# Where GpSimd takes the fifth weight block of a feed-forward period: ahead of the split of the down slot, or behind it

## The chip, the cores and the metric

The kernel runs on one core of one Trainium2 chip. The metric is the device time of one execution in microseconds. Float32 data are used throughout; TensorE multiplies them as pairs of a high and a low part.

## What is computed

Two transformer-like blocks in a row on a 1024 x 1024 activation `x` (tokens x model width). The change lies in the feed-forward part of the first block:

```python
h = rmsnorm(x, norm2_g[l])
u = h @ w_ffn_up[l]                      # 1024 -> 2 x 2816
a, b = u[..., :D_FF], u[..., D_FF:]
a = causal_dwconv(a, ffn_conv_w[l], ffn_conv_b[l])   # three taps
x = x + (jax.nn.silu(a) * b) @ w_ffn_down[l]         # 2816 -> 1024
```

Ahead of it stand an RWKV scan and an mLSTM, behind it the attention layers of the second block. They take most of the span and the change doesn't touch them.

## The kernel before

`build` writes one program per engine; semaphores order them. Data stand transposed, with channels on the 128 partitions. Each fp32 product is made of three matmuls: high part times high part, high times low, low times high. So each weight tile must be split ahead of its use: a copy rounded to the matmul's type is the high part, and the original less the high part is the low part.

The feed-forward part has 22 tiles of 128 hidden channels. Tile 0 is done apart; then come 21 periods, f = 1 to 21 (`FFN_ROWS`). Twenty of them are in loops with four periods per turn (`LOOP_TILES`), the last is written out. In period f TensorE does the up product of tile f (`up_pair`, its matmuls are L1260) and then the down product of tile f-1 (`ffn_down`, L1290).

The up product of a tile (a and b columns together, a 2 x 2 block product) is made with seven half-size products instead of eight (Strassen's scheme). Each of the seven needs one weight block of 128 x 512, which is either a loaded quarter (`upA`, `upB`, two halves each) or a sum or difference of quarters (`unit_sum`). The blocks are called units 0 to 6 in the code. Unit 4, the fifth, is `upB[:, 0, :]`, which holds a difference since line 642 was done. For each unit ScalarE writes the high part (`unit_high`, L2099) and GpSimd the low part (`unit_low`, L630). Both go to a ring of four buffers, so unit 4 goes where unit 0 was, and `unit_high` for unit 4 waits until TensorE is done with product 0. On ScalarE it stands behind `seed` (L2105), which copies bank A to bank B, also after product 0.

TensorE takes the products in the order 0 to 6, 12 matmuls of 512 columns each. It waits for `up_lo` before each of them, for `c_seeded` ahead of product 4 (VectorE's L3088, which itself waits for product 2), and for `ae_added` ahead of product 6 (L3107).

The down weights of a tile (128 x 1024, the "down slot") are loaded to `wraw[:, 1, :]` and split by GpSimd in `down_split`: L662 writes the high part, L664 the low part. `down_split(f)` waits until the down product that used these buffers before is done (`down_done`). That is the last thing that TensorE does ahead of period f's up product. What it writes is used by the down product at the end of period f.

GpSimd's order in period f is: `down_split(f)`, then `later_units(f)` (unit 4, the sum for unit 5 on L653, units 5 and 6), then `first_units(f + 1)` (units 0 to 3 of the next tile, with three sums and differences of the loaded quarters, L640, L642, L644).

VectorE's order in period f: second and third tap of tile f-1's convolution (L3036 and L3039, scalar_tensor_tensor over `apad` and `aconv`), the scaling of b (L3073), the seed of bank C (L3088), the gating product (L3078), the low part of the gated tile (`gL`, L3082), then the exits of banks B, A/E and C (L3101, L3107, L3115), and 16 additions of the down product to `xT` (L2986). ScalarE's order: `seed`, unit 4's high part, SiLU (L2138), `shared_product` (L2111), unit 5's high part, the gated tile's high part `gH` (L2142), unit 6's high part, the next tile's first three, the first tap (L2116), a copy of bank A, the next tile's unit 3.

SyncE's queue issues the loads in a fixed order (`ffn_period`): the down slot once `down_ready` counts the split; half 0 of `upB` once unit 4's low part is done; both halves of `upA` once the sum for unit 5 is done; half 1 of `upB` once unit 6's low part is done.

Of the kernel before, what the change touches and what calls it, by code (L numbers as in the profile page):

```python
# [31 lines left out]
FFN_ROWS = FFN_TILES - 1  # L32
# [92 lines left out]
def build(nc, xin, vec, w_lora, consts, cmask, rope, lnm, band, ws, park, out):  # L125
    with ExitStack() as ctx:
# [11 lines left out]
        def since(name, n):  # L138
            return n + LATER[name][1]

        def sem(name):
            if name in LATER:
                name = LATER[name][0]
            if name not in sems:
                sems[name] = ctx.enter_context(nc.semaphore(name))
            return sems[name]
# [186 lines left out]
        def ring_at(q, u):  # L333

            return (UNITS * q + u) % RING
# [102 lines left out]
        def _(sp):  # L438
# [25 lines left out]
            for j in range(2):  # L464
                rate, keys, power, _, scratch = SETS[j]
                sp.dma_start(AR[:, 0, j, :], keys[:, :]).then_inc(sem("x_moved"), 16)
                sp.dma_start(AR[:, 1, j, :], power[:, :]).then_inc(sem("x_moved"), 16)
                sp.dma_start(BK[:, j, :, CH:3 * CH], rate[:, :].rearrange("p (c x) -> p c x", x=2 * CH)
                             ).then_inc(sem("x_moved"), 16)
                for e in range(2):  # L470
                    sp.dma_start(key_part(j)[:, :, e, :], pairs_of(scratch)[:, :, e, :]).then_inc(sem("x_moved"), 16)
# [67 lines left out]
        def _(pool):  # L539
# [84 lines left out]
            def unit_low(f, q, u):  # L624

                s = ring_at(q, u)
                src = (upA[:, 0, :], unit_sum[s][:, :], upA[:, 0, :], upA[:, 1, :], upB[:, 0, :], unit_sum[s][:, :],
                       upB[:, 1, :])[u]
                pool.wait_ge(sem("up_hi"), since("up_hi", f * UNITS + (u + 1 - UNITS)))
                pool.tensor_tensor(unit_lo[s][:, :], src, unit_hi[s][:, :], ALU.subtract).then_inc(sem("up_lo"), 1)  # L630

            def first_units(f, q):

                n = f * UNITS - UNITS
                unit_low(f, q, 0)
                pool.wait_ge(sem("up_A21"), since("up_A21", f * 16))
                pool.wait_ge(sem("up_A22"), since("up_A22", f * 16))
                pool.wait_ge(sem("up_used"), since("up_used", n + 2))
                s1 = unit_sum[ring_at(q, 1)]
                pool.tensor_tensor(s1[:, :], upB[:, 0, :], upB[:, 1, :], ALU.add).then_inc(sem("up_sum"), 1)  # L640
                pool.wait_ge(sem("up_sum"), since("up_sum", f * 4 - 3))
                pool.tensor_tensor(upB[:, 0, :], upA[:, 0, :], upB[:, 0, :], ALU.subtract).then_inc(sem("up_sum"), 1)  # L642
                pool.wait_ge(sem("up_sum"), since("up_sum", f * 4 - 2))
                pool.tensor_tensor(upA[:, 0, :], s1[:, :], upA[:, 0, :], ALU.subtract).then_inc(sem("up_sum"), 1)  # L644
                unit_low(f, q, 1)
                unit_low(f, q, 2)
                unit_low(f, q, 3)

            def later_units(f, q):

                unit_low(f, q, 4)
                pool.wait_ge(sem("up_used"), since("up_used", f * UNITS - 1))
                pool.tensor_tensor(unit_sum[ring_at(q, 5)][:, :], upA[:, 1, :], upA[:, 0, :], ALU.subtract  # L653
                                   ).then_inc(sem("up_sum"), 1)
                unit_low(f, q, 5)
                unit_low(f, q, 6)

            def down_split(f):

                pool.wait_ge(sem("down_raw"), since("down_raw", f * 16))  # L660
                pool.wait_ge(sem("down_done"), since("down_done", f))
                pool.tensor_tensor(wH[:, 1, :], wraw[:, 1, :], zero, ALU.add).then_inc(sem("down_hi"), 1)  # L662
                pool.wait_ge(sem("down_hi"), since("down_hi", f))
                pool.tensor_tensor(wL[:, 1, :], wraw[:, 1, :], wH[:, 1, :], ALU.subtract).then_inc(sem("down_ready"), 1)  # L664
# [6 lines left out]
            with pool.Fori(0, (FFN_ROWS - 1) // LOOP_TILES) as i:  # L671
                for q in range(LOOP_TILES):
                    f = i * LOOP_TILES + (q + 1)
                    down_split(f)
                    later_units(f, q)
                    first_units(f + 1, q + 1)
            down_split(FFN_ROWS)
            later_units(FFN_ROWS, 0)
            pool.wait_ge(sem("down_raw"), since("down_raw", (FFN_ROWS + 1) * 16))
            pool.wait_ge(sem("up_used"), since("up_used", RING + FFN_ROWS * UNITS - 2))  # L680
# [26 lines left out]
        def _(pe):  # L707
# [803 lines left out]
            def pair_end(br, L, i, first):  # L1511

                _, transposes, values, _ = steps(br, L, i, first)

                def last_block():
                    transposes(7, 0)
                    values(6)

                def values_and_rows():
                    values(7)  # L1520
                    pe.wait_ge(sem("at_rec"), L * 8 + i + (first + 1))
                    pe.transpose(bank(4)[0:16, 0:P], stat[:, S_REC, :], ident).then_inc(sem("at_rows"), 1)

                at = (2, 4, 8) if br == "C" else (3, 6, 11)
                return {at[0]: last_block, at[1]: lambda: transposes(7, 1), at[2]: values_and_rows}
# [231 lines left out]
        def _(act):  # L1757
# [167 lines left out]
            def prepare_powers(j):  # L1925
                _, cum, power, inverse, _ = SETS[j]
                if j == 3:
                    act.wait_ge(sem("rp_done"), 2)
                act.wait_ge(sem("rp_cum"), j + 1)
                act.activation(power[:, :], cum[:, :], ACT.Exp, scale=-DECAY_SCALE).then_inc(sem("rp_exp"), 1)  # L1930
                act.activation(inverse[:, :], cum[:, :], ACT.Exp, scale=DECAY_SCALE).then_inc(sem("rp_exp"), 1)
# [1777 lines left out]
```

## Time and profile before

| what | value |
|---|---|
| median of 3 runs | 3469.43 us (3468.46 to 3472.11) |
| the profiled execution's own time | 3469.67 us |
| its span in the trace | 3467.6 us |
| mean granted TensorE clock | 0.984 of full |
| TensorE busy | 3306.3 us, 95% |
| GpSimd busy | 1395.1 us, 40% |
| VectorE busy | 1931.8 us, 56% |
| ScalarE busy | 927.0 us, 27% |
| L1260, L1290: share of the chain that ended last | 11%, 6% |

The profile is one execution. Its time is the span plus 2.07 us that lie around it. Times in rows are from the span's start. In a timeline a row gives the start, the duration, the engine (PE is TensorE, POOL GpSimd, DVE VectorE, ACT ScalarE, SP SyncE), the line, the operation and its tiles, and in brackets how long the engine idled before and what released it. Matmul durations are modelled and overlap (0.39 us each, started some 0.227 us apart), so TensorE's pace is read from starts.

### The profile page before, as it was taken

The page shows a single profiled execution, that of the slowest core. Times are in us where ns is not written, and L with a number is a line of the kernel's source. Part 1 is how long each engine was busy: PE and PEld are TensorE (multiplying, and loading weights), DVE is VectorE, ACT ScalarE, POOL GpSimd, SP SyncE. Part 2 cuts the span into 40 slices and gives each one's busy share as a digit, 9 for nine tenths or more (in the row PEclk, how much of TensorE's full clock was granted, in tenths as well). Part 3 has the DMA queues.
Part 4 walks back from the last instruction along what each step waited for, and adds up shares of the span by engine and source line. Part 5 has one row for each costly group of instructions (what it writes and reads, how often), then busy time and mean ns, then how long its engine had stood idle before and what let it go on. Part 6 is the DMA issues. An engine that isn't in the chain of part 4 may idle for free.

```text
span 3467.6 us, 55643 instructions
## 1 busy us (share of the span) xinstructions
PE 3306.3 (95%) x22310; PEld 2650.3 (76%) x22310; DVE 1931.8 (56%) x2588; ACT 927.0 (27%) x1515; POOL 1395.1 (40%) x719
## 2 busy tenths in 40 slices
PE   7999788999999999989999999999999999999997
PEld 6878688787888888767777678888776776788886
DVE  7445644558777788855544553443646544443433
ACT  4222343223333333332323320000333322300001
POOL 3323244137777777422222234444322222244444
PEclk9999899999999999999999999999999999999998
DMA  3121100311111111211111121111311111211111
GB/s 138 39 91 44 54 4 4 131 49 37 55 54 54 54 54 51 88 63 52 54 53 43 37 86 49 48 48 49 123 49 50 42 43 49 86 49 49 48 46 63
DMA packets 68390, 198.08 MB, mean 57 GB/s; under 512 B 11409, under 2 KB 22385, under 8 KB 66305
## 3 DMA queue, kind: packets, MB, share of 16 engines
q1 hardware_dynamic: 50880, 140.05, 11.9%
q10 hardware_dynamic: 17344, 55.63, 4.9%
q8 instruction: 128, 2.10, 0.3%
q14 instruction: 38, 0.30, 0.0%
HBM read 167.16 MB, written 16.96 MB: 53 GB/s over the span
## 4 chain that ended last, share of the span: by engine, by line
PE 87%; DVE 7%; issue 2%; ACT 2%; POOL 1%; DMA 1%; ACTq 0%; DVEq 0%; POOLq 0%; SPq 0%
PE ps L723 42%; PE ps L1260 11%; PE ps L1290 6%; PE ps L1662 5%; PE ps L1236 4%; PE ps L1444 3%; PE ps L1471 3%; PE ps L1489 3%; DVE sc L3325 2%; PE ps L1313 1%; PE ps L1035 1%; PE ps L1011 1%; PE ps L1398 1%; PE ps L1103 0%; DVE hL L2659 0%
## 5 line engine op out<-in xcount | busy, mean ns | idle before, releaser
L545 POOL TENSOR_TENSOR wH<-wraw,pv 128x1024 fp32r<-128x1024 f32 x175 | 343.7, 1964 | 1699.1 <-PE ps L723 1423.9
L723 PE MATMUL ps<-hH,wH 128*128 128x512 f32 x2128 | 671.4, 397 | 26.0 <-DVE hL L2659 11.5
L723 PE MATMUL ps<-hL,wH 128*128 128x512 f32 x2128 | 664.1, 393 | 0.0
L723 PE MATMUL ps<-hH,wL 128*128 128x512 f32 x2128 | 663.0, 393 | 0.0
L723 PEld LDWEIGHTS ps<-hH,wH 128*128 128x128 f32 x2128 | 394.6, 189 | 113.4 <-issue 17.8
L547 POOL TENSOR_TENSOR wL<-wraw,wH 128x1024 fp32r<-128x1024 f32 x175 | 461.0, 2634 | 13.8
L723 PEld LDWEIGHTS ps<-hL,wH 128*128 128x128 f32 x2128 | 398.4, 189 | 84.1 <-issue 1.7
L723 PEld LDWEIGHTS ps<-hH,wL 128*128 128x128 f32 x2128 | 398.1, 189 | 82.8 <-issue 0.3
L2986 DVE TENSOR_TENSOR xT<-ps,xT 128x512 f32<-128x512 f32 x544 | 367.2, 690 | 62.8 <-PE ps L1290 53.4
L3428 DVE TENSOR_TENSOR sg<-ps,mrows 128x1024 f32<-128x1024 f32 x46 | 56.3, 1224 | 360.4 <-PE ps L723 360.4
L2300 ACT ACTIVATE sc<-sc,stat 128x256 f32<-128x256 f32 (+7 forms) x256 | 171.1, 669 | 127.4 <-DVE stat L3332 66.4
L2402 ACT ACTIVATE sg<-sg 128x1024 f32<-128x1024 f32 x46 | 48.8, 1061 | 550.0 <-DVE sg L3428 550.0
L1444 PE MATMUL ps<-kP,qP 64*128 64x256 f32 (+3 forms) x672 | 132.7, 492 | 35.2 <-DVE stat L3332 31.5
L1471 PE MATMUL ps<-cst,sc 128*128 128x128 f32 x900 | 149.2, 286 | 12.6 <-ACT pt L2320 8.4
L1471 PEld LDWEIGHTS ps<-cst,sc 128*128 128x128 f32 x900 | 97.2, 141 | 83.5 <-issue 61.4
L1260 PE MATMUL ps<-mixH,unit_hi 128*128 128x512 f32 x336 | 131.7, 392 | 2.7 <-DVE ps L3088 2.7
L1260 PE MATMUL ps<-mixL,unit_hi 128*128 128x512 f32 x336 | 131.4, 391 | 0.0
L1260 PE MATMUL ps<-mixH,unit_lo 128*128 128x512 f32 x336 | 131.2, 391 | 0.0
L1489 PE MATMUL ps<-pt,vtok 128*64 128x128 f32 x1800 | 126.5, 280 | 0.3 <-DVE pt L3349 0.3
L1290 PE MATMUL ps<-gL,wH 128*128 128x512 f32 x320 | 126.4, 395 | 0.0
L1444 PEld LDWEIGHTS ps<-kP,qP 64*128 64x128 f32 x672 | 54.5, 187 | 93.9 <-issue 41.2
L1290 PE MATMUL ps<-gH,wH 128*128 128x512 f32 x320 | 124.5, 389 | 0.0
(502 smaller groups left out, 5901.3 us busy)
## 6 DMA issues: line engine op xcount, KB each, us to landing
wraw<-ws SPq DMA_DIRECT2D x200, 512.0 KB, 3.2
upA<-ws SPq DMA_DIRECT2D x42, 256.0 KB, 2.6
upB<-ws SPq DMA_DIRECT2D x42, 256.0 KB, 2.7
park<-xT ACTq DMA_DIRECT2D x2, 4096.0 KB, 12.8
xT<-park ACTq DMA_DIRECT2D x2, 4096.0 KB, 12.2
recT<-out ACTq DMA_DIRECT2D x28, 256.0 KB, 3.9
xT<-xin SPq DMA_DIRECT2D x4, 1024.0 KB, 8.6
xT<-xin ACTq DMA_DIRECT2D x1, 4096.0 KB, 12.1
```

The lines of the kernel that those rows point to most:

```text
L545: pool.tensor_tensor(wH[:, j, :], wraw[:, j, :], zero, ALU.add).then_inc(w_hi, 1)
L547: pool.tensor_tensor(wL[:, j, :], wraw[:, j, :], wH[:, j, :], ALU.subtract).then_inc(w_ready[j], 1)
L723: mm = pe.matmul(pair(p)[:, half * HALF:(half + 1) * HALF], wp, hp[:, k, half * HALF:(half + 1) * HALF], start=(m == 0 and n == 0), stop=( ...
L1236: mm = pe.matmul(pair(2 + e % 2)[:, half * HALF:(half + 1) * HALF], w[:, j, e * P:(e + 1) * P], h[:, half * HALF:(half + 1) * HALF], start ...
L1260: mm = pe.matmul(bank(b), wp, xp[:, k0 + k, c0:c0 + HALF], start=(start and k == 0 and n == 0), stop=(k == 3 and n == 2), skip_group_check ...
L1290: mm = pe.matmul(pair((2, 3, 1)[e % 3])[:, half * HALF:(half + 1) * HALF], w[:, 1, e * P:(e + 1) * P], h[:, half * HALF:(half + 1) * HALF] ...
L1444: mm = pe.matmul(outs[j][:, c:e], qP[r, n * P:(n + 1) * P], kP[r, k0 + c - c0:k0 + e - c0], start=True, stop=True)
L1471: mm = pe.transpose(out[:, c:c + P], (SC[0] if br == "C" else SC[n % 2])[:, j, b + c:b + c + P], ident)
L1489: mm = pe.matmul(out[r, :], vtok[:, v + 64 * j:v + 64 * j + 64], pt[:, j, b + c:b + c + P], start=(c == c0), stop=(c + P == c1))
L1662: mm = pe.matmul(pair(p)[:, half * HALF:(half + 1) * HALF], wp, hp[:, k, half * HALF:(half + 1) * HALF], start=(k == k0 and n == 0), stop= ...
L2300: act.activation(buf[:, j, b + c0:b + c1], buf[:, j, b + c0:b + c1], ACT.Exp, bias=stat[:, S_NEG, s:s + 1], accum_out=stat[:, S_DEN, s:s + ...
L2986: ins = dve.tensor_tensor(x, bank(2 * pairs[e % len(pairs)] + half), x, ALU.add)
```

## The change

GpSimd's `unit_low(f, q, 4)` leaves `later_units`. It now stands ahead of `down_split(f)`, in the loop and in the last period, which is written out. The order in a period is thus: unit 4, the down split, the sum for unit 5, units 5 and 6, the next tile's first four. No instruction, wait or load is added or removed; the order of the other engines and of the loads is as before.

```diff
--- before.py
+++ after.py
@@ -648,7 +648,6 @@
 
             def later_units(f, q):
 
-                unit_low(f, q, 4)
                 pool.wait_ge(sem("up_used"), since("up_used", f * UNITS - 1))
                 pool.tensor_tensor(unit_sum[ring_at(q, 5)][:, :], upA[:, 1, :], upA[:, 0, :], ALU.subtract
                                    ).then_inc(sem("up_sum"), 1)
@@ -671,9 +670,11 @@
             with pool.Fori(0, (FFN_ROWS - 1) // LOOP_TILES) as i:
                 for q in range(LOOP_TILES):
                     f = i * LOOP_TILES + (q + 1)
+                    unit_low(f, q, 4)
                     down_split(f)
                     later_units(f, q)
                     first_units(f + 1, q + 1)
+            unit_low(FFN_ROWS, 0, 4)
             down_split(FFN_ROWS)
             later_units(FFN_ROWS, 0)
             pool.wait_ge(sem("down_raw"), since("down_raw", (FFN_ROWS + 1) * 16))
```

## Rows read from the trace of the kernel before

**Rows 1.** The page, part 1: busy time and share of the span.

```profile
PE 3306.3 (95%) x22310; PEld 2650.3 (76%) x22310; DVE 1931.8 (56%) x2588; ACT 927.0 (27%) x1515; POOL 1395.1 (40%) x719
```

**Rows 2.** Windows: length, busy time (count) by engine, granted clock, DMA share, GB/s.

```profile
811.50:814.00 2.50, 2.50 (x6) 2.02 (x7) 1.45 (x1) 0.95 (x1) 0.37 (x1) 0.50 0.50 138
832.30:1402.85 570.55, 570.55 (x2510) 470.54 (x2509) 457.79 (x476) 179.23 (x255) 415.68 (x247) 1.00 0.16 53
1689.00:1692.00 3.00, 2.26 (x13) 1.22 (x13) 1.12 (x3) 1.51 (x3) 0.00 (x0) 1.00 0.55 180
```

**Rows 3.** Timeline of the first period: start us, us, engine, line [idle before <-releaser].

```profile
810.57 0.68 DVE L3088 TENSOR_TENSOR ps<-ps,apad 128x512 f32<-128x512 f32 x1
...
811.39 0.79 PE L1260 MATMUL ps<-mixH,unit_hi 128*128 128x512 f32 x1 [2.74 <-DVE ps L3088]
```

**Rows 4.** Timeline of GpSimd over one period.

```profile
1132.60 1.89 POOL L662 TENSOR_TENSOR wH<-wraw,pv 128x1024 fp32r<-128x1024 f32 x1 [4.30 <-PE ps L1290]
1134.57 3.26 POOL L664 TENSOR_TENSOR wL<-wraw,wH 128x1024 fp32r<-128x1024 f32 x1
1137.78 2.28 POOL L630 TENSOR_TENSOR unit_lo<-upB,unit_hi 128x512 fp32r<-128x512 f32 x1
1140.02 2.27 POOL L653 TENSOR_TENSOR unit_sum<-upA 128x512 f32<-128x512 f32 x1
1143.04 1.50 POOL L630 TENSOR_TENSOR unit_lo<-unit_sum,unit_hi 128x512 fp32r<-128x512 f32 x1 [0.74 <-ACT unit_hi L2099]
1145.13 1.81 POOL L630 TENSOR_TENSOR unit_lo<-upB,unit_hi 128x512 fp32r<-128x512 f32 x1 [0.60 <-ACT unit_hi L2099]
...
1150.00 1.29 POOL L640 TENSOR_TENSOR unit_sum<-upB 128x512 f32<-128x512 f32 x1 [1.80 <-DMA upB<-ws]
...
1156.93 1.29 POOL L630 TENSOR_TENSOR unit_lo<-upA,unit_hi 128x512 fp32r<-128x512 f32 x1 [0.36 <-ACT unit_hi L2099]
```

**Rows 5.** Timeline of TensorE: first matmul of product 5 in that period.

```profile
1145.95 0.39 PE L1260 MATMUL ps<-hH,unit_hi 128*128 128x512 f32 x1
```

**Rows 6.** Timeline of ScalarE in the same period.

```profile
1135.35 0.58 ACT L2105 ACTIVATE ps<-ps 128x512 f32<-128x512 f32 x1 [8.44 <-PE ps L1260]
1135.84 0.63 ACT L2099 ACTIVATE unit_hi<-upB 128x512 fp32r<-128x512 f32 x1
...
1142.33 0.63 ACT L2099 ACTIVATE unit_hi<-unit_sum 128x512 fp32r<-128x512 f32 x1 [1.84 <-POOL unit_sum L653]
1143.47 1.06 ACT L2142 ACTIVATE gH<-aconv 128x1024 fp32r<-128x1024 f32 x1 [0.51 <-DVE aconv L3078]
```

**Rows 7.** Timeline of VectorE in the same period.

```profile
1133.16 2.41 DVE L3036 SCALAR_TENSOR_TENSOR aconv<-apad,pv,aconv 128x1024 f32<-128x1024 f32 x1
1135.72 3.18 DVE L3039 SCALAR_TENSOR_TENSOR aconv<-apad,pv,aconv 128x1024 f32<-128x1024 f32 x1 [0.15 <-DVE aconv L3036]
1138.83 2.32 DVE L3073 TENSOR_TENSOR braw<-braw,frows 128x1024 f32<-128x1024 f32 x1
...
1141.67 1.71 DVE L3078 TENSOR_TENSOR aconv<-aconv,braw 128x1024 f32<-128x1024 f32 x1
1144.57 1.23 DVE L3082 TENSOR_TENSOR gL<-aconv,gH 128x1024 fp32r<-128x1024 f32 x1 [1.19 <-ACT gH L2142]
```

**Rows 8.** By line: count, duration ns min/median/max, first and last start us.

```profile
L547 POOL TENSOR_TENSOR wL<-wraw,wH x175: 2338/2393/3489, 6.7 to 3418.9; 128x1024 fp32r<-128x1024 f32 x175
...
L2969 DVE SCALAR_TENSOR_TENSOR hL<-xT,pv,hH x16: 1269/1276/2231, 1439.3 to 2456.2; 128x1024 fp32r<-128x1024 f32 x16
```

**Rows 9.** Timeline of SyncE's queue: the period's last up load is issued.

```profile
1147.11 0.33 SPq L478 DMA_DIRECT2D upB<-ws  x1
```

**Rows 10.** Timeline of TensorE after the last period.

```profile
1433.15 0.77 PE L1313 MATMUL ps<-gH,lastH 128*128 128x512 f32 x1 [5.74 <-DVE gL L3065]
```

**Rows 11.** Timeline of TensorE in the second block's attention.

```profile
1689.04 1.56 PE L1444 MATMUL ps<-kP,qP 64*128 64x512 f32 x8 [1.35 <-DVE stat L3332]
```

## The prediction

> **What bounds the kernel now.** I began with the page. TensorE is busy 95% of the span; GpSimd, whose order the change edits, is busy 40% [rows 1]. So its own busy time decides nothing; what counts is when its results are due. The change sits in the feed-forward loop, so the next view was the loop's stretch: between 832.30 and 1402.85 us TensorE is busy all of the 570.55 us, at full granted clock, 2.4 GHz [rows 2]. That is 19 periods of 30.03 us (f=2 to f=20). TensorE has no gap in them, so nothing can be gained there. A gain could only come from the edges, and the only loop stall next to them is 2.74 us in the first period [rows 3]. A loss can come in any period: as soon as GpSimd delivers one block later than TensorE asks for it.
>
> So I read one period by engine. All times below count from D, when the down product before the period ends and GpSimd is released (1132.55 us, [rows 4]). TensorE's own deadlines: product u of the seven starts 2.72 us after the one before (12 matmuls at some 0.227 us). Product 5 starts at 1145.95, that is D+13.40 [rows 5]; product 6 is then due at D+16.12 and the down product at D+18.84.
>
> GpSimd now [rows 4]: it idles 4.3 to 4.4 us before D; splits the down slot (D+0.05 to D+5.28); then low part of block 4 (to D+7.51), the sum for block 5 (to D+9.74), the low part of block 5 (to D+11.99), that of block 6 (to D+14.39). Block 5 is ready 1.41 us ahead of its deadline. With the 0.14 us that TensorE takes to start after its last releaser (VectorE's seed ends 811.25, TensorE starts 811.39 [rows 3]) the slack is 1.27 us. This is the tightest of them: block 4 is ready at D+7.51 and due at D+10.68.
>
> **The change part by part.** It adds and removes no work. It puts the low part of block 4 ahead of the two instructions of the down split. That low part waits for ScalarE's high part of block 4, which ends at D+3.92 (1135.84+0.63) [rows 6]. It can't be earlier: its ring buffer is block 0's, and ScalarE's seed copy before it waits for product 0 (starts D+2.80). So the move doesn't fill GpSimd's idle time ahead of the split. The two split instructions, which could start at D, now queue behind a wait that ends four microseconds later, and behind them queue block 5's sum, blocks 5 and 6, and the next period's blocks 0 to 3.
>
> The durations need care, since those of [rows 4] are not GpSimd's own. Each long one ends a fixed time after a VectorE instruction: VectorE's second tap ends D+6.35 and block 4's low part ends 1.16 later; its scaling ends D+8.60 and the sum ends 1.14 later; and the other way round, the second tap ends 1.07 after the split's low part, and the scaling 1.09 after block 4 [rows 4, 7]. One of the two engines stands while the other works, where VectorE has both operands in SBUF. Additions that read PSUM (0.68 us) don't lengthen anything. Alone, GpSimd takes 1.28 to 1.29 us for a 512-column block (the sum at 1150.00 in [rows 4]), 1.89 for the split's high part (one operand is a single column) and 2.39 for its low part [rows 8]; VectorE takes 1.28 for a 1024-column scalar_tensor_tensor [rows 8] and 1.23 for a tensor_tensor (gL) [rows 7].
>
> The Trainium skill ("SBUF — State Buffer", section "Who interferes with whom") states the same as a rule: a VectorE instruction with two SBUF inputs and a GpSimd one that reads SBUF exclude each other for the whole instruction. The trace agrees. By that rule the stall comes out as in the sum below; without it, as in the first rival.
>
> Now the new period, step by step:
> - VectorE meets no GpSimd work at first: first tap D+0.61 to D+1.89, 0.15 between, second tap to D+3.32, scaling (1.23) to D+4.51.
> - Block 4's low part is released at D+4.00 (0.08 after ScalarE), stands until D+4.51 and ends 1.15 later, D+5.66.
> - Split: high part D+5.62 to D+7.51 (a following GpSimd instruction shows up 0.04 early), low part, after its semaphore, D+7.59 to D+9.98.
> - Meanwhile VectorE's seed of bank C waits for product 2 (D+8.16) and ends about D+8.9. The gating product (L3078) comes behind it, meets the split's low part, and has waited for a microsecond when that ends. In both handovers of [rows 4, 7] the VectorE instruction that had been waiting went first, so it does here: D+9.98 to D+11.07 (1.09).
> - The sum for block 5 ends 1.14 later: D+12.21, against D+9.74 now.
> - ScalarE starts 0.04 later and takes 0.63: D+12.88. Low part of block 5, 0.08 later, 1.28 alone: D+14.24. TensorE starts product 5 0.14 later: D+14.38 instead of D+13.40.
>
> That is a stall of **0.98 us in a period**: 2.25 us of delay for block 5, less 1.27 us of slack. What is late next: gH and gL, which ScalarE and VectorE do behind block 5's high part (1.06 and 1.23 us [rows 6, 7]), end about D+15.3 (now D+13.25), due at the down product, D+19.8: covered. The addition that frees bank A (ae_added) ends about D+16.6, block 6 about D+16.5; product 6 is due at D+17.1: covered by half a microsecond. On SP's queue stand the down load (behind the split's low part, which ends 4.7 us later) and the four up loads (behind block 4, the sum and block 6, which move by -1.9, +2.5 and +2.1 us; the first of them then waits for the down load's turn instead). The last of them, the second half of B (2.9 us from its issue to GpSimd's use [rows 4, 9]), is the one that GpSimd waits for: it moves from D+14.56 to D+16.6, and the next period's block 3 is done at about D+27.8 instead of D+25.7. Its block 0 is due at D+31.0 and is long done. So nothing accumulates, GpSimd then idles about 7 us ahead of block 4, and each period costs its own 0.98 us again. The down product needs the split at D+19.8; it has it at D+10.
>
> Sum: 19 periods (f=2 to 20) x 0.98 = 18.6 us. The last one (f=21) has VectorE and ScalarE in the chain behind gL (TensorE waits 5.74 us for gL there [rows 10]); b's exit, the first tap half and what follows sit behind gL, so it costs their shift, 2.0 us, and not the stall. The first one (f=1) works against it: without the split in their way VectorE's taps finish earlier and bank C is seeded before its 2.74 us stall, but block 5 is then late in turn, behind the same wait and split. Nothing of this is in the trace; it lies between -4.2 (that stall and 1.45 us of its half clock gone) and +2.0 (like the last period), and I take 0, as the one stall stands for the other. Together **+20.6 us**. Against the profiled execution's 3469.67 that is 3490.3; the median shown is 0.24 us lower, so 3490 us, 0.6% slower. A difference under 0.2% (7 us) is what a measurement of this kernel can't tell from none.
>
> Bounds: GpSimd's and VectorE's durations are from one profile, but which of the two goes first is read from a few handovers. From below: all GpSimd work alone gives block 5 at D+4.00-0.04-0.04+1.28+1.89+0.08+2.39+1.28+0.04+0.63+0.08+1.28 = D+12.87, plus 0.14: no stall. From above: each at its longest of [rows 4] (2.28, 3.26, 2.27, 1.50) gives D+15.95, plus 0.14: a stall of 2.7 us, 21 times: +56 us.
>
> **Rivals.**
> - *The VectorE product doesn't get in between.* If the sum for block 5 follows the split at once (or the two don't exclude each other there), block 5 is ready in time and the slack of [rows 4, 5] takes all of it. For it: the slack is larger than half of the delay. Against: four handovers say that the waiting one goes first. Time 3468 to 3473 us, no change.
> - *The stall lowers TensorE's clock.* In the first period a stall of 2.74 us was followed by some 2.9 us at half clock, 1.2 GHz [rows 2, 3]; per period that would add about 1.45 us, 20 x 2.4 = +49, so 3519 us. Against: a TensorE wait of 1.35 us in a stretch of denser and looser work left the granted clock at 1.00 [rows 2, 11], and ours is shorter. The Trainium skill ("TensorE: Matmul & The Clock Gate", section "HAM oscillation — how this bites in real kernels") warns of a short wait in every tile, repeated; there the waits are longer than this.
> - *Longer exclusion than I worked out* (up to the upper bound): 3502 to 3526 us.
> - *Faster* (the other side): the first period's 2.74 us stall goes, block 5 comes in time there too, and no later period stalls. Price: 2.74 us and the 1.45 us of its half clock, so 3465 us at best. It decides only if the sum ends before D+11.23 in every period. Even then it is under 0.2%.
>
> **How the numbers follow.** Forecast (0.5 to 1.5 us a period, 3480 to 3502 us): 0.78. No stall: 0.11. Lower clock: 0.03. Longer exclusion: 0.06. A gain: 0.02. The range takes in most of the forecast's neighbours and leaves out the no-stall case and the clock: 3476 to 3505 us. Slower by over 0.2% is the forecast, the clock, the longer exclusion: 0.87; within 0.2%: 0.12, which holds nearly all of the gain case too; faster: 0.01.
>
> **What would show it.** In the changed profile, per period: the low part of block 4 waits for ScalarE and starts near D+4, at some 1.7 us; the two taps take 1.3 us each instead of 2.41 and 3.18; the split's low part takes 2.4 us instead of 3.26; L3078 takes over 2 us; the sum ends near D+12.2; TensorE shows a wait for unit_lo (L630) of about 1 us, 19 or 20 times, with the clock at 1.00; the period is 31.0 us. The prediction fails if GpSimd's sum comes ahead of L3078, if VectorE's chain moves so far forward that L3078 runs before the split's low part, or if block 6 or ae_added becomes late as well.

## The result, and the profile after

The changed kernel takes 3495.18 us (median of 4 runs, 3492.97 to 3495.80); the kernel before 3470.77 us (4 runs, 3468.46 to 3472.92). The ratio is 1.007, 95% interval 1.0057 to 1.0083: **24.4 us slower**. The forecast was 3490 us.

The windows of the changed kernel, over the same 19 periods as the second line of [rows 2] (f=2 to f=20), then one stretch of the first period:

```profile
833.70:1426.45 592.75, 576.12 (x2510) 469.09 (x2509) 397.51 (x476) 177.40 (x255) 385.80 (x247) 1.00 0.15 51
816.00:819.00 3.00, 3.00 (x10) 2.30 (x9) 1.81 (x3) 0.63 (x1) 2.95 (x2) 0.55 0.36 117
```

The 19 periods take 592.75 us instead of 570.55, and TensorE now idles in 16.6 of them, at full granted clock. Here is what it waits for, in the view of waits between 790 and 1460 us (waiting line, releaser, total, times, longest):

```profile
PE ps L1261 <- POOL unit_lo L630: 19.9, 21, 2.8
...
PE ps L1314 <- DVE gL L3066: 5.7, 1, 5.7
...
PE ps L1261 <- DVE ps L3089: 1.0, 1, 1.0
```

In the kernel before, GpSimd's low part (L630) was awaited nowhere in these 19 periods; now it is in each. Lines from the edit on are shifted by one, the first few back and the rest forward: the split is L661 and L663, the sum L652, product matmuls L1261, VectorE's gating product L3079.

One ordinary period by engine. D is 1145.79 here (product 0 starts at 1145.59, 0.20 ahead of D as in the kernel before). GpSimd:

```profile
1149.79 1.61 POOL L630 TENSOR_TENSOR unit_lo<-upB,unit_hi 128x512 fp32r<-128x512 f32 x1 [7.27 <-ACT unit_hi L2100]
1151.36 1.89 POOL L661 TENSOR_TENSOR wH<-wraw,pv 128x1024 fp32r<-128x1024 f32 x1
1153.33 2.41 POOL L663 TENSOR_TENSOR wL<-wraw,wH 128x1024 fp32r<-128x1024 f32 x1
1155.68 2.28 POOL L652 TENSOR_TENSOR unit_sum<-upA 128x512 f32<-128x512 f32 x1
1158.70 1.28 POOL L630 TENSOR_TENSOR unit_lo<-unit_sum,unit_hi 128x512 fp32r<-128x512 f32 x1 [0.74 <-ACT unit_hi L2100]
```

VectorE, and under it ScalarE:

```profile
1146.40 1.28 DVE L3037 SCALAR_TENSOR_TENSOR aconv<-apad,pv,aconv 128x1024 f32<-128x1024 f32 x1
1147.83 1.29 DVE L3040 SCALAR_TENSOR_TENSOR aconv<-apad,pv,aconv 128x1024 f32<-128x1024 f32 x1 [0.15 <-DVE aconv L3037]
1149.03 1.22 DVE L3074 TENSOR_TENSOR braw<-braw,frows 128x1024 f32<-128x1024 f32 x1
...
1154.65 2.16 DVE L3079 TENSOR_TENSOR aconv<-aconv,braw 128x1024 f32<-128x1024 f32 x1
1159.61 1.45 DVE L3083 TENSOR_TENSOR gL<-aconv,gH 128x1024 fp32r<-128x1024 f32 x1 [2.79 <-ACT gH L2143]
```

```profile
1149.09 0.62 ACT L2100 ACTIVATE unit_hi<-upB 128x512 fp32r<-128x512 f32 x1
...
1157.99 0.63 ACT L2100 ACTIVATE unit_hi<-unit_sum 128x512 fp32r<-128x512 f32 x1 [6.16 <-POOL unit_sum L652]
```

And TensorE, at product 5:

```profile
1160.04 0.50 PE L1261 MATMUL ps<-hH,unit_hi 128*128 128x512 f32 x1 [0.68 <-POOL unit_lo L630]
```

Read against [rows 4 to 7]: GpSimd idles 7.27 us, until ScalarE's high part of block 4 ends at D+3.92. VectorE's taps, no longer behind the split, fall from 2.41 and 3.18 us to 1.28 and 1.29. The split's low part falls from 3.26 to 2.41 us. But VectorE's gating product, which had to wait for the split's low part (1153.33 to 1155.74), now takes 2.16 us, and the sum behind it 2.28. Block 5's low part ends at 1159.98, TensorE starts at 1160.04, D+14.25 instead of D+13.40. That is 0.85 us at this point; the first matmul behind the wait adds 0.1 (0.33 us to the next start instead of 0.23), and the period is 0.97 us longer. (The row shows 0.68 us of idle and not 0.85, since the modelled duration of the matmul before it reaches past the moment at which the next one would have started.)

The lengths of the periods, from one first matmul of product 0 to the next (from the timelines):

```
period           before   after
f=1              37.48    37.50
ordinary         30.03    31.00    15 of them, f=2 to 20 but for:
f=5, 9, 13, 17   30.02    31.93    the first of each further turn of the loop
f=21 to L1313/4  30.56    32.45    product 0 to TensorE's start after its wait for gL
```

Summed from the traces: 15 x 0.97 + 4 x 1.90 = 22.2 us, the last period 1.9, the first 0.0. That is 24.1 us. The 0.0 is one pair of traces and is worth less than it looks: in the kernels of experiments 9 and 10 below, whose order in the first period is that of the kernel before, this period takes 38.74 and 38.87 us. The spans differ by 25.7, as TensorE enters the first period 1.6 us later in this trace (796.24 against 794.61). The traces of the other kernels below enter it anywhere between 788.7 and 796.2, and nothing ahead of it was changed, so the 1.6 us are no part of the change.

### The profile page after: what moved, and what is told of

Its sections match the earlier page's. It is cut to its first block, busy times and chain, and to the rows that moved or that the text cites. A ratio compares the mean times of both kernels' runs of the same rounds, so it can differ in the third digit from the quotient of the medians.

```text
span 3493.3 us, 55643 instructions
## 1 busy us (share of the span) xinstructions
PE 3313.2 (95%) x22310; PEld 2648.8 (76%) x22310; DVE 1865.9 (53%) x2588; ACT 925.2 (26%) x1515; POOL 1363.4 (39%) x719
## 4 chain that ended last, share of the span: by engine, by line
PE 70%; POOL 11%; issue 9%; DVE 6%; DMA 2%; ACT 2%; POOLq 0%; ACTq 0%; SPq 0%; DVEq 0%
PE ps L724 42%; PE ps L1663 5%; POOL unit_lo L630 4%; PE ps L1237 4%; PE ps L1445 3%; PE ps L1472 3%; PE ps L1490 3%; DVE sc L3326 2%; DMA upB<-ws 1%; POOL wL L663 1%; POOL unit_sum L652 1%; POOL wH L661 1%; PE ps L1314 1%; PE ps L1036 1%; POOL upB L642 1%
## 5 line engine op out<-in xcount | busy, mean ns | idle before, releaser
L630 POOL TENSOR_TENSOR unit_lo<-upB,unit_hi 128x512 fp32r<-128x512 f32 x42 | 75.8, 1804 | 161.0 <-ACT unit_hi L2100 161.0
L1261 PE MATMUL ps<-mixH,unit_hi 128*128 128x512 f32 x336 | 130.9, 389 | 1.0 <-DVE ps L3089 1.0
L1261 PE MATMUL ps<-mixL,unit_hi 128*128 128x512 f32 x336 | 130.7, 389 | 0.0
L1261 PE MATMUL ps<-mixH,unit_lo 128*128 128x512 f32 x336 | 130.7, 389 | 0.0
L1261 PE MATMUL ps<-hH,unit_hi 128*128 128x512 f32 x252 | 102.0, 405 | 25.5 <-POOL unit_lo L630 19.9
```

Source lines behind the costliest of these rows:

```text
L1261: mm = pe.matmul(bank(b), wp, xp[:, k0 + k, c0:c0 + HALF], start=(start and k == 0 and n == 0), stop=(k == 3 and n == 2), skip_group_check ...
```

## The experiments

D and the blocks are as in the prediction. Times are compared with the kernel before on the same chip; the ratio's 95% interval stands in brackets.

**1. Without VectorE's gating product, in the changed kernel.**

```diff
-                dve.tensor_tensor(aconv[:, :], aconv[:, :], braw[:, :], ALU.mult).then_inc(sem("ff_g"), 1)
+                dve.sem_inc(sem("ff_g"), 1)
```

> The changed kernel with VectorE's gating product (silu(a) times b, L3079 there) left out, so the output lacks the factor b; its semaphore is still raised. The split's low part is then followed at once by the sum for block 5. Theory (the stall comes from the late split plus VectorE's product getting in between): the sum ends near D+11.1 instead of D+12.1, TensorE doesn't stall in the ordinary periods (30.03 us each), only in the first one of each loop turn, where ScalarE's table load of 1.28 us delays block 4, by some 0.7 us; in all 4 to 6 us over the kernel before. Rival (the wait for ScalarE alone pushes block 5 past its deadline): the periods stay at 31 us or close to it, 20 us or more over the kernel before.

Measured: 3474.44 us against 3469.42, ratio 1.0016 [1.0006, 1.0026], +5.0 us. Ordinary periods take 30.05 us, the first of a turn 30.95 to 31.00. GpSimd in an ordinary period, its timeline from block 4 to block 5:

```profile
1139.79 1.60 POOL L630 TENSOR_TENSOR unit_lo<-upB,unit_hi 128x512 fp32r<-128x512 f32 x1 [7.51 <-ACT unit_hi L2100]
...
1143.33 2.41 POOL L663 TENSOR_TENSOR wL<-wraw,wH 128x1024 fp32r<-128x1024 f32 x1
1145.69 1.29 POOL L652 TENSOR_TENSOR unit_sum<-upA 128x512 f32<-128x512 f32 x1
1147.72 1.29 POOL L630 TENSOR_TENSOR unit_lo<-unit_sum,unit_hi 128x512 fp32r<-128x512 f32 x1 [0.74 <-ACT unit_hi L2100]
```

The sum takes 1.29 us instead of 2.28, with the split just where the change put it. Block 5's low part ends at 1149.01, D+13.21, and TensorE starts product 5 at D+13.40 as in the kernel before. So the late split alone is absorbed, if barely; it is the split *and* VectorE's product in front of the sum that go past the slack. The rival falls. What is left of the cost lies in the trace in the four first periods of a turn (4 x 0.9 us, see experiment 3) and in the last period (+0.9 us).

**2. The control: the same product left out of the kernel before.** The edit is the same.

> The control: the kernel before with the same product left out. Theory: TensorE has no gap in the periods anyway, so the time is that of the kernel before within 2 us (possibly 1 us less from the first and last period). Rival: if VectorE's product sets a period even in the kernel before, it gets faster by several us.

Measured: 3469.08 us, ratio 1.0 [0.9991, 1.001]. Periods 30.02 and 30.03 us. The product costs the kernel before nothing.

**3. The table loads moved off ScalarE's path, in the changed kernel.** What the prediction missed shows in ScalarE's timeline of the changed kernel in period f=5, the first of a turn:

```profile
929.72 1.28 ACT L2106 ACT_TABLE_LOAD   x1 [7.61 <-PE ps L1261]
931.02 0.58 ACT L2106 ACTIVATE ps<-ps 128x512 f32<-128x512 f32 x1
931.51 0.62 ACT L2100 ACTIVATE unit_hi<-upB 128x512 fp32r<-128x512 f32 x1
932.15 1.28 ACT L2139 ACT_TABLE_LOAD   x1
```

Once in a turn ScalarE loads an activation table ahead of the seed copy and another ahead of SiLU, 1.28 us each. Only the first delays GpSimd. Block 4's low part is released 1.3 us later, but it then no longer meets VectorE's scaling and takes 1.28 us instead of 1.61, so that 0.93 us of delay are left:

```profile
932.21 1.28 POOL L630 TENSOR_TENSOR unit_lo<-upB,unit_hi 128x512 fp32r<-128x512 f32 x1 [8.72 <-ACT unit_hi L2100]
```

The edit puts a SiLU of one column at the head of each turn:

```diff
             with act.Fori(0, (FFN_ROWS - 1) // LOOP_TILES) as i:
+                act.activation(root_col, eps_col, ACT.Silu)
                 for q in range(LOOP_TILES):
```

> The changed kernel with one SiLU of a single column (into a scratch column) at the head of each turn of ScalarE's loop, ahead of the wait for product 0, so that the activation tables are loaded there. Theory (every fourth period is 31.93 us because ScalarE loads a table between product 0 and the seed copy): all periods are 31.00 us, 4 x 0.93 = 3.7 us less than the changed kernel, some 20 to 21 us over the kernel before. Rival (the longer period comes from the jump of GpSimd's or TensorE's own loop): the four periods stay at 31.9 us.

Measured: 3488.55 us against 3469.42, ratio 1.0055 [1.0038, 1.0072], +19.1 us. All periods f=2 to f=20 take 31.00 to 31.04 us, and the trace has one table load in a turn, at its head, where ScalarE would otherwise wait:

```profile
1043.92 1.28 ACT L2201 ACT_TABLE_LOAD   x1
```

So the table load was the cause of the longer first periods of a turn. It is the periods that show this: the intervals of +19.1 and of the changed kernel's +24.4 us overlap.

**4. The control: the same SiLU in the kernel before.**

> The control of the early table load: the kernel before with the same one-column SiLU at the head of each turn of ScalarE's loop. Theory: there the table load lay in ScalarE's idle time and block 4's high part was not awaited by GpSimd, so all periods stay at 30.03 us and the time within 2 us of the kernel before. Rival (the load costs something in itself): several us less.

Measured: 3466.77 us against 3465.86, ratio 1.0002 [0.9993, 1.0011]; periods 30.02 and 30.03. The load costs the periods of the kernel before nothing, though it lies in the same place (timeline of ScalarE, kernel before, f=5):

```profile
925.15 1.28 ACT L2105 ACT_TABLE_LOAD   x1 [8.68 <-PE ps L1260]
...
926.93 0.62 ACT L2099 ACTIVATE unit_hi<-upB 128x512 fp32r<-128x512 f32 x1
```

There block 4's high part ends at 927.55, and GpSimd takes block 4 at 927.63, when the split ends: the slack of 1.3 us on that edge was just enough.

**5. Block 4 between the two instructions of the split**, in the changed kernel. The call ahead of the split goes too (not shown here).

```diff
             def down_split(f, q):
                 pool.tensor_tensor(wH[:, 1, :], wraw[:, 1, :], zero, ALU.add).then_inc(sem("down_hi"), 1)
+                unit_low(f, q, 4)
                 pool.wait_ge(sem("down_hi"), since("down_hi", f))
                 pool.tensor_tensor(wL[:, 1, :], wraw[:, 1, :], wH[:, 1, :], ALU.subtract).then_inc(sem("down_ready"), 1)
```

> The low part of block 4 stands between the two instructions of the down split instead of ahead of both. GpSimd then uses the time before ScalarE is done for the split's high part (1.89 us). Theory: the split's low part ends near D+9.0, VectorE's gating product near D+10.0, the sum for block 5 near D+11.2; TensorE doesn't wait, periods are 30.03 us, and the time is that of the kernel before within 3 us. Rival (any place behind ScalarE's wait is too late): periods of 30.5 us or more, 10 us or more over the kernel before.

Measured: 3470.75 us against 3469.42, ratio 1.0004 [0.9995, 1.0014]. Periods 30.07 us, first of a turn 30.18 to 30.24. GpSimd, D at 1130.48:

```profile
1130.52 1.89 POOL L661 TENSOR_TENSOR wH<-wraw,pv 128x1024 fp32r<-128x1024 f32 x1 [3.53 <-PE ps L1290]
...
1134.47 1.61 POOL L630 TENSOR_TENSOR unit_lo<-upB,unit_hi 128x512 fp32r<-128x512 f32 x1 [2.06 <-ACT unit_hi L2099]
...
1136.05 3.38 POOL L664 TENSOR_TENSOR wL<-wraw,wH 128x1024 fp32r<-128x1024 f32 x1
...
1139.39 2.31 POOL L652 TENSOR_TENSOR unit_sum<-upA 128x512 f32<-128x512 f32 x1
...
1142.44 1.29 POOL L630 TENSOR_TENSOR unit_lo<-unit_sum,unit_hi 128x512 fp32r<-128x512 f32 x1 [0.74 <-ACT unit_hi L2099]
```

The sum ends at D+11.22, at the very edge (D+11.2 was expected). The 1.9 us of work put back into the idle time ahead of ScalarE are what the change lacked. In the trace some 2.4 us are left, 1.0 of them in the last period; the times can't tell that from none.

**6 and 7. The slack, dosed in the kernel before.** The sum for block 5 is made twice (6) or three times (7). The edit of 6:

```diff
+                pool.tensor_tensor(unit_sum[ring_at(q, 5)][:, :], upA[:, 1, :], upA[:, 0, :], ALU.subtract).then_inc(sem("pool_own"), 1)
+                pool.wait_ge(sem("pool_own"), f * 1 + (1 + MASK_STEPS - 0))
                 pool.tensor_tensor(unit_sum[ring_at(q, 5)][:, :], upA[:, 1, :], upA[:, 0, :], ALU.subtract
                                    ).then_inc(sem("up_sum"), 1)
```

> The kernel before (old order) with the sum for block 5 made twice, one after the other, in each of the 21 periods: 1.28 us more on GpSimd between block 4 and block 5, and a semaphore (0.08 us). It measures the slack of block 5 without any of the change. Theory with exclusion: VectorE's gating product goes in between the two sums, so the second ends at D+11.97 instead of D+9.74; block 5 is 2.2 us late against a slack of 1.3 to 1.4: periods of 30.7 to 30.9 us, +15 to +18 us. Rival (no exclusion: only the 1.36 us of added work count): the slack takes it, +0 to +2 us.

> The same with the sum made three times. Theory: the third sum meets no VectorE work and adds its own 1.28+0.08 us; block 5 is 3.6 us late, TensorE stalls 2.1 us a period: +42 to +48 us if its clock stays at 2.4 GHz. Rival on the clock: a stall of 2.1 us in every period drops the granted clock to half for a while each time, as 2.74 us did in the first period: +70 us or more.

Measured, one more: 3485.45 us against 3470.33, ratio 1.0039 [1.0025, 1.0053], +15.1 us; periods 30.81 to 30.89 us. Two more: 3538.27 us, ratio 1.0191 [1.0169, 1.0213], +68 us; periods of 33.8 us and of 32.17 us. With one more sum, GpSimd and VectorE in the timeline:

```profile
1149.09 2.26 POOL L653 TENSOR_TENSOR unit_sum<-upA 128x512 f32<-128x512 f32 x1
...
1150.73 1.70 DVE L3080 TENSOR_TENSOR aconv<-aconv,braw 128x1024 f32<-128x1024 f32 x1
...
1151.43 2.15 POOL L655 TENSOR_TENSOR unit_sum<-upA 128x512 f32<-128x512 f32 x1
...
1154.33 1.28 POOL L630 TENSOR_TENSOR unit_lo<-unit_sum,unit_hi 128x512 fp32r<-128x512 f32 x1 [0.74 <-ACT unit_hi L2101]
```

VectorE's product starts at 1150.73, stands until the first sum ends (1151.35) and ends 1.08 later, 1152.43; the second sum stands behind it and ends 1.15 after that. The added work is 1.36 us, but the sum ends 2.2 us and more later than in the kernel before. Against the period's D (1141.55) block 5's low part ends at D+14.06 instead of D+11.99, and TensorE starts product 5 at D+14.11 instead of D+13.40:

```profile
1155.66 0.50 PE L1262 MATMUL ps<-hH,unit_hi 128*128 128x512 f32 x1 [0.55 <-POOL unit_lo L630]
```

Of 2.07 us of delay 0.71 reach TensorE, so the slack is 1.36 us. With two more sums TensorE's wait is 1.85 us, and the windows right behind it are:

```profile
1051.50:1054.00 2.50, 2.50 (x7) 1.92 (x7) 0.83 (x2) 0.07 (x1) 2.02 (x2) 0.50 0.18 48
1055.00:1060.00 5.00, 5.00 (x23) 4.12 (x22) 2.26 (x4) 1.41 (x3) 4.68 (x4) 1.00 0.00 0
```

The granted clock is at half, 1.2 GHz, shortly after the stall and then full again. Of the periods f=2 to f=20, fourteen take 33.8 us each, 1.6 us more than the five of 32.17 us, which are longer than 30.03 by the stall alone (2.14 us). The five are f=2, 5, 10, 15 and 20. The theory had the stall right (2.1 us) and the clock wrong; the rival on the clock holds, and the total lies close to it.

**8. The sum for block 5 ahead of the split as well.**

```diff
                     unit_low(f, q, 4)
+                    fifth_sum(f, q)
                     down_split(f)
...
```

`fifth_sum` is the sum, taken out of `later_units`; the last period is changed alike (neither is shown here).

> The changed kernel with the sum for block 5 ahead of the down split too: block 4, sum, split, blocks 5 and 6. ScalarE then has block 5's high part early, but its low part on GpSimd still stands behind the split. Theory: split's low part ends near D+11.2, VectorE's gating product near D+12.3, block 5's low part near D+13.4: a stall of 0.1 to 0.2 us in ordinary periods and some 1.4 us in the first of a turn, 5 to 10 us over the kernel before. Rival (the sum and ScalarE's hop are what make block 5 late, not the split): no stall at all, within 2 us of the kernel before.

Measured: 3484.24 us against 3470.33, ratio 1.0043 [1.0029, 1.0057], +13.9 us: more than both theories. Ordinary periods take 30.23 us as expected, but the first of a turn 32.04 to 32.09. The timeline of f=5 shows a second VectorE instruction getting in between (its own row numbers: L666 is the split's low part, L3084 the gating product, L3088 gL):

```profile
928.06 1.89 DVE L3084 TENSOR_TENSOR aconv<-aconv,braw 128x1024 f32<-128x1024 f32 x1
...
928.95 3.27 POOL L666 TENSOR_TENSOR wL<-wraw,wH 128x1024 fp32r<-128x1024 f32 x1
...
931.14 2.17 DVE L3088 TENSOR_TENSOR gL<-aconv,gH 128x1024 fp32r<-128x1024 f32 x1 [1.19 <-ACT gH L2148]
...
932.17 2.26 POOL L630 TENSOR_TENSOR unit_lo<-unit_sum,unit_hi 128x512 fp32r<-128x512 f32 x1
```

The table load shifts GpSimd by 0.9 us, so that the gating product goes ahead of the split's low part, gL is asked for while that runs, and goes ahead of block 5. TensorE's wait there (1.72 us) left its clock alone. The trace has 11.2 us more in the loop and 1.3 us in the last period. The first period takes 39.05 us, near the 38.74 and 38.87 us of kernels whose order there is unchanged, so its 1.6 us can't be put down to the edit.

**9. The last period alone.** The order in the loop is that of the kernel before.

> One part of the change alone: block 4 ahead of the down split only in the last period, which is written out; the loop keeps the old order. Theory: the periods in the loop stay at 30.03 us, the last period costs 1.9 us (gL is late by that), +1.9 us in the profile. Rival: the last period's cost is hidden or grows (0, or more than 4 us).

Measured: 3472.31 us against 3470.33, ratio 1.0003 [0.9993, 1.0013], which can't be told from none; in the trace the loop's periods are 30.02 and 30.03 us, and the last one, from product 0 to the start after the wait for gL, takes 32.47 us instead of 30.56: +1.9. The first period, which the edit doesn't touch, takes 38.74 us here against 37.48: TensorE's wait for bank C's seed is 3.06 us instead of 2.74, and the half clock behind it lasts longer.

**10. The same exclusion in the tail, turned to use.** TensorE waits 5.74 us for gL after the last period [rows 10]. Ahead of it, VectorE's instructions with both operands in SBUF run beside GpSimd's split for the second block. The edit, on the kernel before, has that split wait:

```diff
                     if L == 0 and n == 0:
                         pool.wait_ge(sem("down_done"), since("down_done", FFN_ROWS))
+                        pool.wait_ge(sem("row_lo"), FFN_TILES + 1)
```

> The kernel before with one wait more: GpSimd takes the first weight slot of the second block only after VectorE has made gL of the last tile. In the tail of the feed-forward part VectorE is on the chain that ended last and its instructions with both operands in SBUF wait for that split (1.78 and 2.88 us instead of 0.7 and 0.75). Theory of exclusion: two of them get 1.1 and 2.1 us shorter, TensorE's wait for gL falls from 5.7 us to some 2.5 to 3 us, the time by 3 us (0.1%); the split still ends before TensorE asks for it, 19 us later. Rival: the wait for gL stays at 5.7 us, or the deferred split is late in turn and the time rises.

Measured: 3463.36 us against 3465.86, ratio 0.9989 [0.998, 0.9998]: faster than the kernel before, by 2.5 us of the medians and 0.1% by the ratio, with an interval that just leaves out no gain. Two of VectorE's instructions there, before (first fence) and with the edit (second):

```profile
1422.93 1.78 DVE L3055 TENSOR_TENSOR braw<-braw,frows 128x512 f32<-128x512 f32 x1
1424.63 2.88 DVE L3045 SCALAR_TENSOR_TENSOR aconv<-apad,pv,aconv 128x512 f32<-128x512 f32 x1
```

```profile
1418.44 0.68 DVE L3056 TENSOR_TENSOR braw<-braw,frows 128x512 f32<-128x512 f32 x1
1419.41 0.75 DVE L3046 SCALAR_TENSOR_TENSOR aconv<-apad,pv,aconv 128x512 f32<-128x512 f32 x1 [0.28 <-ACT aconv L2126]
```

```profile
1425.80 0.59 PE L1314 MATMUL ps<-gH,lastH 128*128 128x512 f32 x1 [2.86 <-DVE gL L3066]
```

TensorE's wait falls from 5.74 to 2.86 us.

## Why the prediction was right

- **TensorE bounds the loop, and block 5 is the tightest delivery.** Right: the only new wait in the loop is for L630, ahead of product 5. Experiment 6 shows it in the old order too: of 2.07 us of delay 0.71 reach TensorE, so the slack is 1.36 us (1.27 was worked out; TensorE starts 0.06 us behind GpSimd, not 0.14).
- **The move gives GpSimd no idle time to fill, but takes it from the split.** Right: block 4 starts at D+4.00 to the hundredth. Experiment 5 gives the time back for the high part alone, and all but some 2 us of the loss is gone.
- **VectorE and GpSimd exclude each other, and the waiting one goes first.** Right: each end lies within 0.05 us of the forecast (split D+9.95, gating product D+11.02, sum D+12.17, block 5 D+14.19, against 9.98, 11.07, 12.21, 14.24). Experiment 1 settles it by cause. The first rival (no exclusion there) is what the changed kernel would be without the gating product. The Trainium skill ("SBUF — State Buffer", section "Who interferes with whom") says that issue order decides who blocks. The trace of experiment 8 agrees: with GpSimd 0.9 us later, VectorE's gating product was there ahead of the split's low part instead of behind its start, and the period took 1.8 us longer than an ordinary one.
- **0.98 us a period.** Measured 0.97 in 15 of 19, but that it is so near is in part luck: TensorE starts product 5 0.85 us late and not 0.98 (0.08 us less from GpSimd's end to its start, 0.05 from the ends before), and the slow first matmul behind the wait, 0.1 us, was no term of the sum.
- **What it missed** is a term of the sum: it took the period at 1132 us for all 19, and four of them cost 1.90 us, since ScalarE's table load lies between product 0 and block 4's high part once in a turn. That is 4 x 0.93 = 3.7 us, and it is most of the distance from +20.6 to +24.4. The load stood in the trace of the kernel before; its price only appears once GpSimd waits on that edge. Experiments 3 and 4 show it. It is the traces that show the miss: the measured difference reaches from 19.8 to 28.8 us by its interval and takes in the forecast +20.6.
- **The first period at 0.** Measured +0.02 us, and that is luck, as this period alone differs by more than 1 us between kernels with the same order in it (37.48, 38.74 and 38.87 us). What happened in it: the old 2.74 us wait for bank C's seed fell to 1.0, and a new one of 2.8 us for block 5 came; behind it the clock was at half, as the second window of the changed kernel shows (0.55).
- **The last period at 2.0.** Measured 1.9 (experiment 9 too).
- **The clock rival** did not come true at 0.68 to 1.61 us of idle TensorE, but it is nearer than the prediction said. It was weighed with a wait of 1.35 us that did no harm, as if the length of the wait decided; experiment 7 has 1.85 us in a dense stretch drop the clock in 14 periods out of 19, and experiment 4's kernel has a wait of 3.15 us that didn't (rows at the end).

## What to carry to other kernels

When an instruction with a late releaser is put at the head of an in-order engine, count what it holds up, not what it does: here one block of 1.3 us held back 4.3 us of split that had been free to run in idle time. Then read the gap to the next deadline with the neighbour engine's instructions in it, since on GpSimd and VectorE the order in which they meet decides what is added. And look at more than one period of a loop: one in four had a table load that only the changed order exposed.

## What the runs showed of the hardware that was not expected

- The granted clock of TensorE fell to half behind waits of 1.85 us in 14 of 19 periods (+1.6 us each), but not behind 1.61 (4 of 4, changed kernel) nor 1.72 us (4 of 4, experiment 8) in the same stretch of matmuls. In the other five periods with 1.85 us the clock stayed full and nothing was lost; they come at regular distances (f=5, 10, 15, 20, and f=2). In the first period waits of 2.74, 2.92 and 3.06 us for bank C's seed were followed by half clock (kernel before, experiments 10 and 9), one of 3.15 us was not (experiment 4's kernel, rows below: the wait, then the window behind it), and its first period takes 36.04 us. So the length of the wait alone doesn't decide; what does stays open.

```profile
808.33 0.49 PE L1260 MATMUL ps<-mixH,unit_hi 128*128 128x512 f32 x1 [3.15 <-DVE ps L3089]
808.40:813.00 4.60, 4.60 (x21) 3.79 (x22) 3.41 (x4) 2.10 (x3) 1.77 (x2) 1.00 0.25 75
```

- ScalarE loads its activation tables anew in the first period of each loop turn (2 x 1.28 us), though the three periods behind it use the same functions without a load. With a one-column SiLU at the head of the turn the trace has one load in a turn instead of two, out of the path (experiment 3).
- VectorE's and GpSimd's durations obey the same arithmetic over the whole loop, before, after and in experiments 3, 4 and 8: the one that stood ends 1.07 to 1.10 us (VectorE, 1024 columns, alone 1.22 or 1.28) or 1.12 to 1.18 us (GpSimd, 512 columns, alone 1.28) after the other.
